# Fused two-block model, one core: the matmuls of two heads alternate in one piece, and the guests of the second input product are spaced anew

## The reference, cut to what matters

```
Lmat = jnp.exp(segsum(adt))
cb = jnp.einsum('bctgn,bcsgn->bgcts', Cc, Bc)
y_diag = jnp.einsum('bgrcts,bcsgrp->bctgrp', cb[:, :, None] * Lmat, X)
```

```
drive_r = jnp.einsum('bsgh,gph->bsgp', ug, bbar_r)
drive_i = jnp.einsum('bsgh,gph->bsgp', ug, bbar_i)
_, _, h_r, h_i = lax.associative_scan(_complex_linear_combine, elems, axis=1)
y = (jnp.einsum('bsgp,ghp->bsgh', h_r, c_re.astype(f32))
     - jnp.einsum('bsgp,ghp->bsgh', h_i, c_im.astype(f32)))
```

```
s = jnp.einsum('bqhd,bkhd->bhqk', qi, k) * scale
s = s + ci[..., None] - c_keys
s = jnp.where(k_pos[None, :] <= q_pos[:, None], s, -jnp.inf)
p = jax.nn.softmax(s, axis=-1)
return jnp.einsum('bhqk,bkhd->bqhd', p, v)
```

## Time and profile before

| what | value |
|---|---|
| median of 3 runs | 1678.33 us (1677.52 to 1679.55) |
| the profiled execution | 1679.45 us |
| its span | 1677.7 us |
| PE busy | 1603.7 us (96%) |
| DVE busy | 1157.2 us (69%) |
| ACT busy | 793.4 us (47%) |
| out of the first recurrence, L1976 | 64 records, 17.2 us |
| drive of the scan, L2919 | 64 records, 18.0 us |
| out of the scan, L2932 | 128 records, 31.9 us |
| scores and values of the forget attention, L3375 and L3396 | 32 and 32 records, 9.0 and 8.6 us |

### The profile page before, as it was taken

One profiled execution on the slowest core, in us unless ns is written; L12 is line 12 of the kernel. 1 busy time (PEld: TensorE's weight loads), 2 busy tenths in 40 slices (PEclk: granted clock), 3 DMA queues, 4 the chain that ended last, 5 costly groups with the idle time before them and its releaser, 6 DMA issues.

```text
span 1677.7 us, 23127 instructions
## 1 busy us (share of the span) xinstructions
PE 1603.7 (96%) x9280; PEld 1353.9 (81%) x9280; DVE 1157.2 (69%) x1825; ACT 793.4 (47%) x1079; POOL 58.8 (4%) x72
## 2 busy tenths in 40 slices
PE   8988999998999999999999998999999999899998
PEld 6788876678998888987799887866775678789997
DVE  5787766449986675776687566898863585466653
ACT  4555564444543354545354533656524544444442
POOL 0000000000000000000000003430020000000000
PEclk9988999999999999999999999999999999999999
DMA  9884442324867734433555553422332344245542
GB/s 391 297 322 155 183 191 94 116 105 174 343 236 306 299 148 151 151 126 126 201 201 226 178 197 105 149 90 96 131 110 76 151 151 151 76 151 184 193 176 75
DMA packets 41369, 292.86 MB, mean 175 GB/s; under 512 B 4528, under 2 KB 4784, under 8 KB 6704
## 3 DMA queue, kind: packets, MB, share of 16 engines
q1 hardware_dynamic: 40112, 284.04, 45.6%
q10 hardware_dynamic: 1152, 7.34, 1.1%
HBM read 288.22 MB, written 3.15 MB: 174 GB/s over the span
## 4 chain that ended last, share of the span: by engine, by line
PE 74%; DVE 16%; ACT 5%; issue 3%; DMA 2%; POOL 1%; DVEq 0%; ACTq 0%; SPq 0%; POOLq 0%
PE ps L1032 32%; PE ps L1040 27%; DVE ring_at_lo L1221 5%; ACT w_hi L1210 2%; DMA ring_at<-stream 2%; DVE arena_at L1135 1%; PE ps L2932 1%; PE ps L2471 1%; DVE arena_at L2050 1%; PE ps L999 1%; PE ps L3142 1%; PE ps L1976 1%; PE ps L2229 1%; PE ps L2919 1%; PE ps L2202 1%
## 5 line engine op out<-in xcount | busy, mean ns | idle before, releaser
L1221 DVE TENSOR_TENSOR ring_at_lo<-ring_at,w_hi 128x2048 fp32r<-128x2048 f32 (+1 forms) x218 | 495.2, 2274 | 202.5 <-ACT w_hi L1210 202.3
L1210 ACT ACTIVATE w_hi<-ring_at 128x2048 fp32r<-128x2048 f32 (+1 forms) x218 | 414.3, 1903 | 222.4 <-PE ps L1032 132.9
L1040 PE MATMUL ps<-h_hi,w_hi 128*128 128x256 f32 x1440 | 414.3, 288 | 3.7 <-DVE hT_at_lo L1485 2.5
L1040 PE MATMUL ps<-h_hi,ring_at_lo 128*128 128x256 f32 x1440 | 415.2, 288 | 0.0
L1040 PE MATMUL ps<-hT_at_lo,w_hi 128*128 128x256 f32 x1440 | 410.3, 285 | 0.0
L1032 PE MATMUL ps<-w_hi,arena_at_lo 128*128 128x512 f32 x1232 | 390.5, 398 | 2.8 <-DVEq L4277 0.8
L1040 PEld LDWEIGHTS ps<-h_hi,w_hi 128*128 128x128 f32 x1440 | 278.0, 193 | 14.9 <-issue 14.4
L1032 PEld LDWEIGHTS ps<-w_hi,arena_at_lo 128*128 128x128 f32 x1232 | 229.4, 189 | 58.8 <-issue 6.9
L1040 PEld LDWEIGHTS ps<-h_hi,ring_at_lo 128*128 128x128 f32 x1440 | 276.4, 192 | 0.0
L1040 PEld LDWEIGHTS ps<-hT_at_lo,w_hi 128*128 128x128 f32 x1440 | 274.0, 190 | 0.3
L1032 PE MATMUL ps<-ring_at_lo,arena_at_lo 128*128 128x512 f32 x616 | 244.1, 396 | 0.0
(11 more groups left out here) (457 smaller groups left out, 1685.9 us busy)
## 6 DMA issues: line engine op xcount, KB each, us to landing
ring_at<-stream SPq DMA_DIRECT2D x266, 1024.0 KB, 4.9
arena_at<-bias ACTq DMA_DIRECT2D x4, 768.0 KB, 6.0
kept<-arena_at ACTq DMA_DIRECT2D x2, 1024.0 KB, 10.7
arena_at<-kept ACTq DMA_DIRECT2D x2, 1024.0 KB, 7.5
arena_at<-mem SPq DMA_DIRECT2D x1, 1024.0 KB, 7.3
x_res<-x SPq DMA_DIRECT2D x1, 1024.0 KB, 17.1
out<-x_res SPq DMA_DIRECT2D x2, 512.0 KB, 2.8
con<-consts SPq DMA_DIRECT2D x1, 640.0 KB, 23.1
```

Source lines behind the costliest of these rows:

```text
L1040: mm = pe.matmul(k.ps[:, bank + q // 2, (q % 2) * TOK:(q % 2 + 1) * TOK], w[:, q * P:(q + 1) * P], x, start=first and n == 0 and q % 2 == ...
L1210: act.activation(k.w_hi[:, s % HI, 0:n, :], k.ring[:, c % RING, 0:n, :], ACT.Identity).then_inc(k.hi_done, 1)
L1221: dve.tensor_tensor(k.w_lo[:, c % RING, 0:n, :], k.ring[:, c % RING, 0:n, :], k.w_hi[:, s % HI, 0:n, :].bitcast(F32), ALU.subtract).then_i ...
```

## The change

**Pairs.** In the first recurrence, the scan and the forget attention, the matmuls of two heads (tiles) are issued in one piece, and they alternate: first s (or part and c, or t) of the even one, the same of the odd one, then the next. The two write or read different partitions: halves of the array in the recurrence and the attention, two of four quarters in the scan. The waits of the odd one now stand ahead of the piece: `weights_in` 2p+2, `s5_turned_in` 2i, `s5_turned_out` 2i+4, `probs_in` h, `probs_taken` h+2. Each still raises its own semaphore. In the scan the drives of tiles i and i+1 stand at even steps, and the outs of tiles i-3 and i-2 at odd ones; DVE's rotated outputs have three buffers in place of two, and a rotation waits for `s5_used` of the tile three back. In the attention scores of two heads stand at even steps and values of two heads at odd ones; the turns stay single.

**Spacing** in `in2`:

```diff
-        Woven(k, in2, (Threaded(gate), paced([(0, 3, 8, 14)])), (Threaded(s5_stage), paced([(0, 21, 12, 60)])),
-              (Threaded(hg_prep), paced([(0, 1, 49, 50), (1, 3, 50, 58)])),
-              (Threaded(hgrn), paced([(0, 21, 60, 88)])),
-              (Threaded(prep), paced([(0, 6, 88, 96)])),
-              (Threaded(fox), paced([(0, 11, 96, 116)], True))),
+        Woven(k, in2, (Threaded(gate), paced([(0, 3, 8, 14)])), (Threaded(s5_stage), paced([(0, 21, 12, 70)])),
+              (Threaded(hg_prep), paced([(0, 1, 56, 57), (1, 3, 57, 66)])),
+              (Threaded(hgrn), paced([(0, 21, 70, 94)])),
+              (Threaded(prep), paced([(0, 6, 94, 100)])),
+              (Threaded(fox), paced([(0, 11, 100, 116)], True))),
```

The core of the rest (the first recurrence's out, then the scan's drive and out, the third buffer, and the attention):

```diff
-        def out(h):
-            pe.wait_ge(*m["weights_in"].at(h + 1))
-            if h >= 2 and h % 2 == 0:
-                pe.wait_ge(*m["head_taken"].at(h // 2))
-            if h == 0:
+        def out(p):
+            pe.wait_ge(*m["weights_in"].at(2 * p + 2))
+            if p >= 1:
+                pe.wait_ge(*m["head_taken"].at(p))
+            else:
                 pe.wait_ge(*m["offsets_taken"].at(1))
-            rows = slice(HP * (h % 2), HP * (h % 2) + HP)
             for s in range(2):
-                mm = pe.matmul(k.ps[rows, 6, 0:TOK], self.xt[:, s, h * HP:(h + 1) * HP],
-                               self.e[:, h % 3, s * TOK:(s + 1) * TOK], start=s == 0, stop=s == 1)
-            mm.then_inc(m["head_out"].sem, 1)
+                for h in (2 * p, 2 * p + 1):
+                    rows = slice(HP * (h % 2), HP * (h % 2) + HP)
+                    mm = pe.matmul(k.ps[rows, 6, 0:TOK], self.xt[:, s, h * HP:(h + 1) * HP],
+                                   self.e[:, h % 3, s * TOK:(s + 1) * TOK], start=s == 0, stop=s == 1)
+                    if s == 1:
+                        mm.then_inc(m["head_out"].sem, 1)
...
             if i >= 2:
-                pe.wait_ge(*m["s5_turned_in"].at(2 * i - 2))
-            rows = slice(32 * j, 32 * j + 32)
+                pe.wait_ge(*m["s5_turned_in"].at(2 * i))
+            q = i // 4
             for c in range(2):
-                mm = pe.matmul(k.ps[:, 4 + i % 2, c * TOK:(c + 1) * TOK], self.bT[rows, c, q * P:(q + 1) * P],
-                               self.uT[rows, q, :], start=True, stop=True)
-            mm.then_inc(m["s5_drive"].sem, 1)
+                for j in (i, i + 1):
+                    rows = slice(32 * (j % 4), 32 * (j % 4) + 32)
+                    mm = pe.matmul(k.ps[:, 4 + j % 2, c * TOK:(c + 1) * TOK], self.bT[rows, c, q * P:(q + 1) * P],
+                                   self.uT[rows, q, :], start=True, stop=True)
+                    if c == 1:
+                        mm.then_inc(m["s5_drive"].sem, 1)
...
-            pe.wait_ge(*m["s5_turned_out"].at(2 * i + 2))
+            pe.wait_ge(*m["s5_turned_out"].at(2 * i + 4))
             for n, part in enumerate((self.h, self.b2)):
                 for c in range(2):
-                    mm = pe.matmul(k.ps[32 * j:32 * j + 32, 6 + q % 2, 0:TOK], self.cs[:, c, i, :],
-                                   part[:, i % 2, c * TOK:(c + 1) * TOK], start=n + c == 0, stop=n + c == 2)
-            mm.then_inc(m["s5_used"].sem, 1)
+                    for e in (i, i + 1):
+                        rows = slice(32 * (e % 4), 32 * (e % 4) + 32)
+                        mm = pe.matmul(k.ps[rows, 6 + q % 2, 0:TOK], self.cs[:, c, e, :],
+                                       part[:, e % 3, c * TOK:(c + 1) * TOK], start=n + c == 0, stop=n + c == 2)
+                        if n + c == 2:
+                            mm.then_inc(m["s5_used"].sem, 1)
...
-            if i < S5T:
+            if i < S5T and i % 2 == 0:
                 drive(i)
-            if 2 <= i < S5T + 2:
-                out(i - 2)
+            if 3 <= i < S5T + 2 and i % 2:
+                out(i - 3)
...
-            if i >= 2:
-                dve.wait_ge(*m["s5_used"].at(i - 1))
+            if i >= 3:
+                dve.wait_ge(*m["s5_used"].at(i - 2))
...
             for t in range(TT):
-                mm = pe.matmul(bank[:, t * TOK:(t + 1) * TOK], self.qkT[rows, h // 2, t * P:(t + 1) * P],
-                               self.qkT[rows, 4 + h // 2, :], start=False, stop=True, skip_group_check=True)
-            mm.then_inc(m["scores_in"].sem, 1)
+                for g in (h, h + 1):
+                    rows = slice(64 * (g % 2), 64 * (g % 2) + 64)
+                    mm = pe.matmul(k.ps[:, 4 + g % 2, t * TOK:(t + 1) * TOK],
+                                   self.qkT[rows, g // 2, t * P:(t + 1) * P], self.qkT[rows, 4 + g // 2, :],
+                                   start=False, stop=True, skip_group_check=True)
+                    if t == TT - 1:
+                        mm.then_inc(m["scores_in"].sem, 1)
...
-            if 2 <= h <= FOXH + 1:
-                values(h - 2)
+            if 3 <= h <= FOXH + 1 and h % 2:
+                values(h - 3)
```

More of the change, by code:

```diff
@@ L1984, in tensor @@
             args(h, 1)
-            if h >= 1:
-                out(h - 1)
+            if h >= 2 and h % 2 == 0:
+                out(h // 2 - 1)
             yield
-        out(NH - 1)
+        out(NH // 2 - 1)
         yield
@@ L2909, in drive @@
         def drive(i):
-            q, j = i // 4, i % 4
             if i == 0:
@@ L3389, in values @@
         def values(h):
-            pe.wait_ge(*m["probs_taken"].at(h + 1))
-            if h >= 2 and h % 2 == 0:
+            pe.wait_ge(*m["probs_taken"].at(h + 2))
+            if h >= 2:
                 pe.wait_ge(*m["heads_hi"].at(h // 2))
                 pe.wait_ge(*m["heads_lo"].at(h // 2))
-            rows = slice(64 * (h % 2), 64 * (h % 2) + 64)
             for s in range(2):
-                mm = pe.matmul(k.ps[rows, 7, 0:TOK], self.v[:, s, h * 64:(h + 1) * 64], self.pt[:, h % 2, s, :],
-                               start=s == 0, stop=s == 1)
-            mm.then_inc(m["heads_out"].sem, 1)
+                for g in (h, h + 1):
+                    rows = slice(64 * (g % 2), 64 * (g % 2) + 64)
+                    mm = pe.matmul(k.ps[rows, 7, 0:TOK], self.v[:, s, g * 64:(g + 1) * 64], self.pt[:, g % 2, s, :],
+                                   start=s == 0, stop=s == 1)
+                    if s == 1:
+                        mm.then_inc(m["heads_out"].sem, 1)
         pe.wait_ge(*self.prep.m["fox_qk"].at(4))
@@ L3404, in tensor @@
         for h in range(FOXH + 3):
-            if h < FOXH:
+            if h < FOXH and h % 2 == 0:
                 scores(h)
@@ L3999, in block2_stages @@
     ab = s5w.take(2, 2, 512)
-    g, h, b2 = s5w.take(1, 512)[:, 0, :], s5w.take(2, 512), s5w.take(2, 512)
-    assert gla.at <= at_gl + 6 * D
+    g, h, b2 = s5w.take(1, 512)[:, 0, :], s5w.take(3, 512), s5w.take(3, 512)
+    assert gla.at <= at_gl + 6 * D and s5w.at <= SPARE
     hw = region(k, work)
```

23 lines of the change are left out of this document (12 added, 11 removed).

## The result

The kernel after takes 1659.19 us (median of 4 runs, 1658.79 to 1662.27), beside 1678.94 us for the kernel before on the same chip: a ratio of 0.9881, 95% interval 0.9857 to 0.9905. The forecast was 1657. Its profiled execution took 1658.79 us, its span is 1657.0, so 20.7 us less than the span of before.

The account below looks back on a forecast made before the run. The prediction took PE's queue to bound the touched places, DVE nearly so in the scan and second recurrence. Work -34.5, waits +5.5, +1.5, +1.4, +2.5 and clock +1.7 sum to -21.9 us, giving 1657 us (range 1645 to 1679).

Parts of the forecast that it names:

- likeliest case: Whole kernel: the prediction's own forecast of 1657 us, chance 0.52, alone spanning 1650 to 1664 us.
- two big terms: Whole kernel: 34.5 us less work in PE's queue, against waits given back, 10.9 us in the second product.
- I take 5: First recurrence's out pairs: eight trace matmuls cost 5 slots of 0.22 us, between bounds 4 and 8; saves 7.9 us.
- everything overlaps: Rival for all paired pieces: 4 slots of 8, the scan gaining nothing since DVE ends last; 1654 us, chance 0.10.
- Scan's waits: Scan: DVE becomes longer than PE, which waits 7.9 us for turned_out where it waited 2.4; +5.5 us (2 to 8).
- Second recurrence: Second recurrence: about as much idle as before, with less to cover ACT's exponentials; +1.5 us (0 to 4).
- Turned queries: Before the turned queries: one quarter less between out and fillers, so PE's idle of 1.17 us becomes 2.6; +1.4 us.
- Forget attention: Forget attention waits: sixteen quarters where there were twenty, a short gap for the pair's second head; +2.5 us (0 to 5.6).
- Waits together: Second product: added PE waits of scan +5.5, second recurrence +1.5, turned queries +1.4 and forget attention +2.5 us.
- Clock: Place not named: one more 3.41 us stretch at the 1.2 GHz level after idle, costing half of itself; +1.7 us.
- Waits of over 25 us in the second product: Sign of being wrong: PE's waits in the second product summing to over 25 us.
- Drains at A/B changes: Rival inside paired pieces: each of 128 changes between A and B drains PE 0.18 us, 23 us; 1700 us, chance 0.08.

Follow-up runs that it names:

- grouped kernel: Kernel after with each pair still one piece, but all matmuls of the first head ahead of those of the second: 1667.9 us, ratio 0.9908 to before.
- the spacing alone: Kernel before with only the new spacing of the guests among the main product's quarters, no pairs: 1678.0 us beside 1683.8, ratio 0.9966.
- the old spacing: Kernel after, all pairs kept, with the spacing of before (scan over 48 quarters of the main product in place of 58): 1665.6 us, ratio 0.9891 to before.
- single heads: Kernel after with the forget attention head by head as before, in its new place (quarters 100 to 116): 1664.5 us, ratio 0.9895 to before.
- the first recurrence alone: Kernel before with pairs in the first recurrence only: 1676.1 us, ratio 0.9951 to before.

## Why the prediction came out right, and what in it was wrong

The time was right (1657 for 1659.2) and so were the likeliest case and the places. Its two big terms were both too small, and cancelled: 7.1 us more work went than forecast, 3.7 us more waiting came in the second product, and 5.4 us of idle ahead of it that the forecast did not have. That the sum came within 2 us is luck in part.

- **Overlap: the step "I take 5".** The assumption that a matmul's two passes stay in line, with B's first behind A's second, failed. The order is A1 B1 A2 B2, 4 slots of 8 and 8 of 16: the lower bound of each term. By these slots the work removed is 9.7 + 23.6 + 8.3 = 41.6 us, not 34.5. PE's busy time fell by 40.6, and that holds 1.7 of added half clock. The case "everything overlaps" had 0.10 of the chance and was the truth on the mechanism; its time of 1654 was missed because its waits were mis-sized as mine were. The grouped kernel shows it: there a piece of A A B B in program order takes four slots, and it would take six if B waited for A's second matmul to start. The Trainium skill, "TensorE: Matmul & The Clock Gate", Part 3, says that matmuls start and end strictly in program order; for fp32 matmuls in different parts of the array the traces here disagree, and decide. Its rule that such neighbours run together, some 4 ns apart, holds in the main: the starts are 6 to 7 ns apart here.
- **Scan's waits.** Mechanism right (DVE over 95% busy: 104.3 of 108 us; PE's waits for L3043), size wrong: 12.3 us where I had 7.9. 3.2 of the 4.4 are the first error: 47 quarters, eight drive pairs and seven outs at four slots of eight make 65.8 + 9.9 + 14.0 = 89.7 for PE in place of 92.9. And DVE's sum was short: from first to last rotation 105.1 us for 99.4. Of these 5.7 us, 3.0 are idle for drives, which the forecast put at none; 0.9 come from a misread row (of the 8.0 us of idle before, 0.97 lie ahead of the first rotation, so DVE's work was 95.1 and not 94.2); and 1.8 are additions, scans and rotations that were a little slower. The splits were ten before and twelve after, where nine and eleven had been counted; the difference of two was right. PE's sum was longer too by the 3.4 us that 6.8 us of half clock cost it, and that much of DVE's excess did not become waiting. So the scan got hardly shorter (108.2 for 108.8), though it holds 47 quarters from its first drive to its last out where it held 39. DVE's splits and first rotations from 1053 to 1162 us, against the earlier trace rows (count, busy us, mean ns, idle before; 0.97 of the 3.6 lies ahead of the first rotation):

```profile
L1221 DVE TENSOR_TENSOR ring_at_lo<-ring_at,w_hi 128x2048 fp32r<-128x2048 f32 x12 | 27.6, 2299 | 0.3 <-ACT w_hi L1210 0.3
...
L3017 DVE TENSOR_TENSOR arena_at<-ps,arena_at 128x512 f32<-128x512 f32 x16 | 10.9, 682 | 3.6 <-PE ps L2922 3.6
```

- **Second recurrence.** Forecast +1.5; it waits 2.1 us less, and already did so with the spacing alone.
- **Turned queries.** Forecast +1.4, the idle there at 2.6; measured 1.9 for the 1.2 of the earlier trace rows, so +0.7.
- **Forget attention.** Forecast +2.5, measured +5.7, at the outer bound (5.6) that I had set with one quarter a pair. The chain has one step of one and a half quarters at the odd head's place; a later turn takes the waits away.
- **Waits together:** 10.9 forecast for the second product, 14.6 measured (24.9 for 10.3), and 1.5 in the first recurrence's heads, where I had none. Waits of over 25 us in the second product were to be a sign of being wrong; its five stages idle for 24.9.
- **Clock.** One more stretch of 3.41 us forecast, +1.7. After has 44.4 us at half clock and before 41.0 (13 and 12 times 3.41, each without the stretch at the very end), so just that; the second trace of after has 47.8. As the sum of more and fewer at other places this was luck. Two of after's stretches. The first begins at the end of an idle time of 3.67 us before an out (1095.89 to 1099.56), the second 1.0 us behind one of 3.66 us before a turn of the forget attention:

```profile
1098.97:1102.38 3.41, 2.82 (x14) 1.29 (x16) 3.41 (x6) 1.96 (x5) 0.59 (x1) 0.50 0.02 5
1279.88:1283.29 3.41, 3.41 (x13) 2.08 (x10) 0.87 (x4) 2.08 (x7) 0.00 (x0) 0.50 0.00 0
```

- **Drains at A/B changes:** none. Sixteen matmuls with fifteen changes take 1.85 us, as eight without one. The Trainium skill, "TensorEngine Tiling (Array Packing)", Key Properties, says that only a change of mode drains TensorE. On this it held: a change of tile within a mode costs nothing here.

By the sum: -41.6 of work, 14.6 of idle time in the second product, 5.4 in the first two stages of the table and 1.7 of clock make -19.9; the spans differ by 20.7. Of the 5.4 the recurrence's heads have 1.5. The other 3.9 lie ahead of them, in code that the change doesn't touch. 2.6 are in the stretch from the start to the first recurrence, which idles 13.5 to 17.6 us in the traces of this study and does so whatever the kernel (14.0 with the old spacing, 13.5 with single heads). 1.3 are one wait of PE at 151 us for DVE's L1135, 5.9 us in before, with the spacing alone and with the first recurrence alone, and 6.5 to 7.2 us in all kernels with the pairs of the second block. Why is open for both.

## What to carry to other kernels

Matmuls that use half or a quarter of the array are worth pairing wherever they come in heads: in the 256-column fp32 pieces here two cost one, if no more than two matmuls of the first stand ahead of the second's, and no strict alternation is needed. The gain arrives only where the engines behind PE have room and each head's chain has enough steps until its next matmul, so lengthen that lag when pairing. Read the granted clock beside every wait that is left, since half clock costs on top of the wait: 13.7 us of it in the scan cost 4.8 us of the stage.

## What the runs showed of the hardware

- The two passes of neighbouring fp32 matmuls into different parts interleave: pairs of starts 6 to 7 ns apart, 216 ns from pair to pair of 256 columns (240 to 320 behind the first of a piece), for parts by result columns (64 and 32) and by rows (32 and 64) alike.
- TensorE's queue lets a later matmul start first: past four passes of two older matmuls, one of them under way (13 or 14 ns behind it), not past eight (the first of B started 6 ns behind A's fifth pass). The piece took four slots of eight in the first case, twelve of sixteen in the second.
- One program's traces differ in their stretches at 1.2 GHz: after had 10.2 and 20.5 us of them from 1040 to 1310 us in two traces, and other kernels of nearly the same work up to 30.7. Nineteen fillers in three idle gaps removed all 13.7 us that one stage had, and the stage went from 110.9 to 106.1 us.
